# Streamed columns, additions per coefficient step and the order of dilated weight groups in a kernel of four layers

## What is computed

```python
fq, fk, fv, fg, dq, dk, dv = split(rms_norm(h) @ w_in)
fox_o = forgetting_attention(fq, fk, fv, fg + forget_bias)        # 16 heads of 64
dil_o = dilated_attention(rope(dq), rope(dk), dv)                 # 16 heads of 64
h = h + concat(rms_norm(fox_o), rms_norm(dil_o)) @ w_out
q = (hn @ w_query).reshape(T, 8, 2, 128)                          # hn = rms_norm(h)
scores = einsum('thpc,hpnc->thpn', q, sub_keys)                   # 128 keys for each half
...                                                               # best 16 pairs (i1, i2) of each of 8 heads
experts = i1 * 128 + i2                                           # 128 experts for each token
u = take(expert_down, experts); hdn = gelu(einsum('ted,td->te', u, hn))
y = einsum('te,ted->td', gates * hdn, take(expert_up, experts))
out = rms_norm(h + y)
```

## Time and profile before

| | us |
|---|---|
| median of three runs | 3365.07 |
| the three runs | 3365.07, 3355.38, 3365.72 |
| profiled execution | 3357.47 |
| its span | 3355.6 |
| TensorE busy in the span | 2604.7 (78%) |
| VectorE busy | 2260.8 (67%) |
| ScalarE busy | 1014.9 (30%) |
| GpSimd busy | 829.3 (25%) |
| HBM traffic | 255 GB/s mean |

### The profile page before, as it was taken

One profiled execution on the slowest core, in us unless ns is written; L12 is line 12 of the kernel. 1 busy time (PEld: TensorE's weight loads), 2 busy tenths in 40 slices (PEclk: granted clock), 3 DMA queues, 4 the chain that ended last, 5 costly groups with the idle time before them and its releaser, 6 DMA issues.

```text
span 3355.6 us, 34774 instructions
## 1 busy us (share of the span) xinstructions
PE 2604.7 (78%) x13316; PEld 2045.2 (61%) x13316; DVE 2260.8 (67%) x3034; ACT 1014.9 (30%) x1651; POOL 829.3 (25%) x581
## 2 busy tenths in 40 slices
PE   3789999998989999799999893000097029999998
PEld 3689999987879877798887793000064016544443
DVE  6777777776755455443544558999999984566666
ACT  2133434343444444443335540000086014200000
...
DMA  8767777776856534365342455999999993699998
GB/s 292 250 226 256 268 266 255 265 247 215 279 176 171 145 113 140 94 183 150 112 121 76 139 164 241 371 359 349 357 421 421 422 368 113 240 409 410 409 409 332
DMA packets 340693, 858.35 MB, mean 256 GB/s; under 512 B 38072, under 2 KB 97728, under 8 KB 306864
## 3 DMA queue, kind: packets, MB, share of 16 engines
...
HBM read 853.95 MB, written 2.10 MB: 255 GB/s over the span
## 4 chain that ended last, share of the span: by engine, by line
PE 38%; DVE 13%; DMA 12%; POOL 9%; issue 3%; ACT 1%; DVEq 0%; ACTq 0%; POOLq 0%
DMA s<-in_up_rows,s 11%; PE ps L1718 10%; PE ps L1719 10%; PE ps L1720 10%; POOL s L627 9%; DVE s L1663 7%; PE ps L2226 2%; DVE s L1676 1%; PE ps L2204 1%; PE ps L2202 1%; PE ps L2095 1%; DMA s<-in_peer_down,s 1%; PE ps L1979 1%; POOL s L639 1%; PE ps L2097 1%
## 5 line engine op out<-in xcount | busy, mean ns | idle before, releaser
L1718 PE MATMUL ps<-r,r 128*128 128x256 f32 (+2 forms) x3248 | 1064.7, 328 | 76.2 <-DVE r L1066 45.0
L1066 DVE TENSOR_TENSOR r<-s,r 128x1024 fp32r<-128x1024 f32 (+1 forms) x532 | 649.6, 1225 | 588.8 <-ACT r L654 588.5
L1719 PE MATMUL ps<-r,r 128*128 128x256 f32 (+2 forms) x3248 | 1045.5, 322 | 0.0
L1720 PE MATMUL ps<-r,r 128*128 128x256 f32 (+2 forms) x3248 | 1045.2, 322 | 0.0
L654 ACT CAST r<-s 128x1024 fp32r<-128x1024 f32 (+1 forms) x532 | 551.3, 1039 | 916.6 <-PE ps L1720 870.3
L1718 PEld LDWEIGHTS ps<-r,r 128*128 128x128 f32 x3248 | 640.4, 197 | 130.6 <-DVE r L1066 43.0
L1719 PEld LDWEIGHTS ps<-r,r 128*128 128x128 f32 x3248 | 640.4, 197 | 42.7 <-issue 4.5
L1720 PEld LDWEIGHTS ps<-r,r 128*128 128x128 f32 x3248 | 639.4, 197 | 40.8
L1663 DVE CUSTOM_DVE_ANT_0 s<-s,s 128x2048 f32<-128x2048 f32 x256 | 583.7, 2285 | 30.6 <-DMA s<-in_peer_down,s 30.3
L627 POOL DMA_INDIRECT s<-in_peer_down,s x256 | 472.8, 1847 | 398.5 <-DVE s L1621 187.9
L1676 DVE SCALAR_TENSOR_TENSOR s<-s,s,s 128x1024 f32<-128x1024 f32 x256 | 328.5, 1283 | 164.9 <-DMA s<-in_up_rows,s 163.2
...
...
## 6 DMA issues: line engine op xcount, KB each, us to landing
...
s<-in_ret_w_in SPq DMA_DIRECT2D x128, 512.0 KB, 5.2
s<-in_up_blocks SPq DMA_DIRECT2D x128, 512.0 KB, 6.8
...
s<-in_ret_w_in SPq DMA_DIRECT2D x128, 256.0 KB, 3.9
...
```

Of the source, the lines that this page charges most:

```text
L1066: v.tensor_tensor(lo_of(w), raw_of(w), hi_of(w).bitcast(F), ALU.subtract).then_inc(*lo_made.to(w))
L1718: pe.matmul(o, lh, rh, start=start, stop=False, skip_group_check=True)
L1719: pe.matmul(o, lh, rl, start=False, stop=False, skip_group_check=True)
L1720: return pe.matmul(o, ll, rh, start=False, stop=stop, skip_group_check=True)
```

## The change

**Experts.** DCOL goes from 1024 to 896: each up gather brings 1152 columns for 1024, each block 896, in matmuls of 448. There are five gather buffers for six; four block buffers stay, and both sets lie elsewhere: two block buffers lie where the indices were, so the first blocks wait for the indices' rounded and transposed copies, and the first two gather buffers lie in the selection's scratch. For t = 1 the comparison is made for the first index alone. The second index is transposed once for the tile and negated into SECOND, and ScalarE makes OH2 from it and a table of 0 to 127 with four small activations a step. Two additions go with a step.

**Dilated groups.** They are computed in the order 0, 2, 4, 1, 3, 5. X rounds call next once each, and L rounds 0 to 7 once each, two units a round. The four turns move to L rounds 8 and 9, two each, and the 16 O3 units to rounds 9 to 20, one or two each.

```diff
@@ constants and buffers @@
-DCOL = 1024
-NU = 6
+DCOL = 896
+HCOL = DCOL // 2
+NU = 5
...
-        EFR = [at(kept_end + 256 * t, 2, 128, of=arena_r) for t in range(2)]
+        EFR = [at(kept_end + 256 * t, 2 - t, 128, of=arena_r) for t in range(2)]
+        SECOND = at(kept_end + 384, 128)
...
-        ubuf = [at(144 * KB + 1024 * i, D - DCOL) for i in range(2)] + [at(YG + 1024 * i, D - DCOL) for i in range(4)]
-        sbuf = [at(W + 4096 + DCOL * i, DCOL) for i in range(NS)]
+        ubuf = [at(W + 4096 + (D - DCOL) * i, D - DCOL) for i in range(2)] + [at(YG + (D - DCOL) * i, D - DCOL) for i in range(3)]
+        sbuf = [at(144 * KB + DCOL * i, DCOL) for i in range(2)] + [at(W + 8192 - DCOL * i, DCOL) for i in (2, 1)]
...
+        DIL_ORDER = (0, 2, 4, 1, 3, 5)
...
-        for g in range(6):
+        for g in DIL_ORDER:
             cols512(w2, 3088 + g * 512)
...
+        def fox_units(i):
+
+            each = (0,) * 9 + (1, 2, 1, 2, 1, 2, 1, 2, 1, 1, 1, 1)
+            return range(sum(each[:i]), sum(each[:i + 1])) if 0 <= i < 21 else ()
@@ sync @@
             sp.wait_ge(*gate_made.at(1))
+            sp.wait_ge(*picks_rounded.at(1))
+            sp.wait_ge(*second_copied.at(0))
             for b in range(128):
@@ gpsimd @@
+            g.wait_ge(*gate_made.at(1))
             for n in range(256):
                 i, t, j = n % NU, n // 128, n % 128
-                if n == 0:
-                    g.wait_ge(*picks_rounded.at(1))
-                elif n == 2:
+                if n == 2:
                     g.wait_ge(*rows_used.at(255))
@@ scalar: dilated part @@
-            for i in range(21):
+            for i in range(22):
                 if i < 16:
                     exps("L", i)
                 if 0 <= i - 1 < 16:
                     flip_copy("L", i - 1)
+                if i < 8:
+                    next(work)
                 if i == 1:
                     mix_part(0)
-                if 2 <= i < 6:
-                    turn("O", i - 2, colA[:, 88:104], None, HT)
-                if i >= 6:
-                    cast(O3 + 4 + i - 6)
+                if i in (8, 9):
+                    for _ in work:
+                        pass
+                    turn("O", 2 * i - 16, colA[:, 88:104], None, HT)
+                    turn("O", 2 * i - 15, colA[:, 88:104], None, HT)
+                for u in fox_units(i - 1):
+                    cast(O3 + 4 + u)
@@ scalar: experts @@
             for t in range(2):
+                if t:
+                    s.wait_ge(*second_turned.at(0))
+                    s.mul(SECOND, bank[5][:, 0:128], -1.0).then_inc(*second_copied.to(0))
...
-                        s.wait_ge(*compared.at((t, q)))
-                        if 32 * t + q >= 2:
-                            s.wait_ge(*built.at(fours[32 * t + q - 2]))
-                        if t == 0:
+                        if t:
+                            s.wait_ge(*second_copied.at(0))
+                            s.wait_ge(*built.at(fours[30 + q]))
+                            for k in range(4):
+                                c = 4 * q + k
+                                r = s.activation(OH2[q % 2][:, k, :], STEP, ACT.Abs, bias=SECOND[:, c:c + 1])
+                            r.then_inc(*less_read.to((t, q)))
+                        else:
+                            s.wait_ge(*compared.at((t, q)))
+                            if q >= 2:
+                                s.wait_ge(*built.at((0, q - 2)))
                             s.activation(flat(o1), bank[q % 2], ACT.Abs)
-                        s.activation(o2, bank[2 + q % 2], ACT.Abs).then_inc(*less_read.to((t, q)))
+                            s.activation(o2, bank[2 + q % 2], ACT.Abs).then_inc(*less_read.to((t, q)))
@@ vector: experts @@
-                if 2 <= n < 34:
-                    q = n - 2
+                if n % 2 and n // 2 - 1 in range(32):
+                    q = n // 2 - 1
@@ tensor: dilated part @@
                     next(work, None)
                 if 0 <= i - 1 < 16:
                     flip("X", i - 1)
-                if i < 16 and i % 2:
-                    next(work, None)
                 if i >= 2:
                     attend("X", i - 2, FV)
-            for _ in work:
-                pass
-            pe.wait_ge(*rotated.at(("D", 7)))
-            pe.wait_ge(*dv_copied.at((1, 1)))
...
             for i in range(21):
+                if i in (0, 8):
+                    if i:
+                        for _ in work:
+                            pass
+                    pe.wait_ge(*rotated.at(("D", 7 if i else 3)))
+                    pe.wait_ge(*dv_copied.at((i // 8, 1)))
                 if i < 16:
                     scores_of("L", i, DQ, DK)
+                if i < 8:
+                    next(work)
...
-                if 2 <= i < 6:
-                    turn("O", i - 2, O, lambda t, k: mix_normed.at((t, 0)))
-                if i >= 5:
-                    out_unit(O3 + i - 5, (i - 5) // 4, (i - 5) % 4)
+                if i in (8, 9):
+                    turn("O", 2 * i - 16, O, lambda t, k: mix_normed.at((t, 0)))
+                    turn("O", 2 * i - 15, O, lambda t, k: mix_normed.at((t, 0)))
+                for u in fox_units(i):
+                    out_unit(O3 + u, u // 4, u % 4)
@@ tensor: experts @@
-                for p in range(2):
+                for p in range(2 - t):
                     b = 2 * p + q % 2
...
             for t in range(2):
+                if t:
+                    take(5)
+                    pe.transpose(bank[5][:, 0:128], EF[1][:, 1, :], IDN).then_inc(*second_turned.to(0))
+                    free[5] = second_copied.at(0)
                 compare(t, 0)
...
-                        r = pe.matmul(bank[2 * t + b], coef_of(t, i2), sbuf[i2 % NS][:, b * 512:(b + 1) * 512],
+                        r = pe.matmul(bank[2 * t + b][:, 0:HCOL], coef_of(t, i2), sbuf[i2 % NS][:, b * HCOL:(b + 1) * HCOL],
                                       start=i2 == 0, stop=i2 == 127)
```

75 lines of the change are left out of this document (37 added, 38 removed).

## The result

The changed kernel takes 3310.35 us (median of 4 runs, 3309.86 to 3310.61) against 3364.36 (median of 4 runs, 3355.38 to 3365.72): ratio 0.9845, interval 0.9828 to 0.9862. It is 54 us faster, and the time lies inside the forecast's range.

A forecast was written before the change was run, and what follows sets the result against it. Two chains were taken to end together: TensorE's blocks and gathers in the remaining DMA bandwidth. Parts one to three -57 us, part four -5: span 3293.6, plus 2 and 3.5, predicted 3299 us; range 3281 to 3334.

The forecast's parts named there:

- Part one: Coefficient steps: 4.60 us falls to 3.46, set by VectorE, TensorE next at 3.16; dense product starts 27 us earlier.
- GpSimd ... is done in 2.8: Coefficient step: GpSimd's two gather issues need 0.94 us each, and even at a 1.39 pace end in 2.8 us.
- the 2 us granted for refilling: Coefficient steps: 2 us added to 31 x 3.46 = 107 us for refilling five gather buffers.
- Part two: Dense product: TensorE's block shrinks from 3.43 to 3.00 us, 384.5 us for 128, ending at 3260.
- Part three: Up gathers: 2.30 us each beside blocks, 1.65 for the last 19; last addition about 3283 instead of 3339.6.
- rival 4: Up gathers: rows of 4608 bytes travel as two packets, 20 us added, 3319 us in all; chance 0.05.
- Part four: Dilated groups: spread units fill the sparse stretch at the first L heads; -5 us taken, bounds -12 and +12.
- Rival 5: Dilated groups: spread units cost instead of giving, by more frequent half clock in X; 3312 us, chance 0.07.
- The 3.5 us added: Whole kernel: 3.5 us added to 3295.5, since the profiled execution lay 8 us below the median of three runs.
- The sum: Whole kernel: 3355.6-57-5 = 3293.6 us span, 2 us around it, 3295.5 for an execution like the profiled one.
- rival 6: After the blocks, additions at 1.5 us, dilated groups give 12: 3290 us, or 3283 with more GB/s; chance 0.06.

The follow-up runs named there:

- e3: Changed kernel with one addition per coefficient step instead of two: 3346.05 us.
- e2: Kernel before with only the dilated groups' new order put in, experts untouched: 3354.85 us, ratio to before 0.9974.
- e10: Changed kernel with 928 streamed columns, first_hot cut in halves, and two of the first four blocks loaded ahead of the new waits: 3283.58 us, ratio to before 0.9766.
- e8: Changed kernel with 928 streamed columns instead of 896, nothing else: 3292.52 us, ratio to before 0.9789.
- e1: Changed kernel with the dilated groups in their old order, experts' change kept: 3321.15 us, ratio to before 0.9875.

## Why the prediction was right, and where it was off

**Part one.** TensorE's step without the second comparison: forecast 3.16, e3 shows 3.09. (The 4.60 us from which it was worked out was one step; the mean of the 31 before was 4.48. The working's 2752.1+30x4.6+1 meets the 2891 read in the trace although there are 31 steps.) VectorE's 3.46 is in the trace to the hundredth, but only in steps without a wait; the mean is 3.71. The step that failed is "GpSimd ... is done in 2.8": it took the pace of six additions in a row, 1.39 us, as GpSimd's pace, while in the changed kernel an issue takes 1.45 us and 0.30 follow, 3.5 in all, so that there is almost no reserve to make up for a late landing. Its row stood in the earlier trace rows: in 2455 to 2727 us GpSimd is busy 238.14 us for 110 issues, 2.17 us each and not 0.94, beside VectorE's products of the down rows. Price: 31 x 0.25 less the 2 us granted for refilling, 6 us on both chains.

**From the last step to the dense product** it took 10.9 us, not the 9.4 of before: the gain matmuls (2872.98, above) took 7.16 us. They took 7.16 or 7.17 in the other twelve kernels' traces too, also behind steps without a gap (e3) and with the experts of before (e2). The execution profiled of before is the exception:

```profile
2895.59 4.94 PE L2234 MATMUL ps<-s 16*128 16x128 f32 x32 [0.94 <-ACT s L1003]
```
```profile
2894.60:2898.00 3.40, 2.46 (x22) 2.44 (x22) 3.19 (x3) 0.65 (x2) 2.71 (x3) 1.00 0.58 164
```

The granted clock was 1.00 for these 3.4 us there, and 0.50 in every other trace. So the forecast took a lucky 9.4 for the rule; from the last first_hot to these matmuls the changed kernel takes 0.8 us less (3.77 instead of 4.54), so that 1.5 us are left of the 2.2.

**Part two.** Right: blocks of 3.007 us, 387.4 us for all where 386.5 were forecast, clock 1.00, TensorE 25 us ahead of the gathers (23 forecast).

**Part three.** Right in kind: 409 GB/s, landing 9.7, an end set by the gathers alone. From the last step to the last addition 423.7 us where 419 were forecast. The pace beside the blocks is right: 163 additions in 376.0 us, from the first block streamed again (2885.7) to the landing of the last (3261.7), are 2.31 each, 2.30 forecast. The two ends, where the gathers have the DMA engines alone, were mis-sized: 9 additions in the 16.5 us after the last step, 1.8 each instead of 1.6, and 18 in 31.2 us behind the last block's landing, 1.74 instead of 1.65, again with issues of 1.2 to 2.1 us (3276.09, above). And the last block landed 5.8 us before TensorE's end, not 9. Of these 18 additions, 14 come after TensorE's end, where some 20 were forecast. Rows of 4608 bytes were not cut: 20,912 packets of that queue in 2900 to 3235 us, for 146 gathers of 128 rows and their closing packets (a ninth), so rival 4 falls.

**Part four.** The trace gives 4.9 us for X and L together (298.3 us instead of 303.2 from X's first scores to L's last product), 5 were forecast. Of these 3.1 were lost again before the first addition. About half, 1.4 us, lies between L's last product and the first product of the down rows, which is 197.5 us or more in every trace with the new order and 195.9 and 196.3 in the two with the old one. The other 1.7 us lie in the stretch of the down rows, by the blocks now loaded at 2575 us in full DMA traffic. The forecast had put that load at nothing; e10, which loads two of the four at 2393 us, has that stretch 1.9 us shorter than e8. In the new order X and L took 298.3 or 298.4 us in each of the twelve traces; in the old one 303.2 in the execution of before and 310.8 in e1's, where 217 us of X ran at a clock of 0.92 and of 0.88:

```profile
1554.00:1771.00 217.00, 217.00 (x1291) 186.14 (x1291) 92.60 (x181) 75.56 (x137) 0.00 (x0) 0.92 0.39 114
```
```profile
1554.00:1771.00 217.00, 217.00 (x1253) 186.34 (x1252) 89.76 (x179) 73.08 (x133) 0.00 (x0) 0.88 0.36 107
```

That would explain why the groups are worth 8.7 to 10.8 us against the median, while only 1.6 us lie between the profiled executions of before and e2 (3357.5 and 3355.8): the profiled one of before lay 7 us under the median. It isn't shown, since no median execution of before was profiled. Nor does the new order make all executions alike: the changed kernel's four lie within 0.8 us, but e2's eleven spread over nearly 9 us and e3's four over 7.3, and 10 was the spread of before. Rival 5 did not come: the clock in X was 0.91 or 0.92 in the new order. The 3.5 us added to come from the profiled execution to the median were too much: the changed kernel's profiled execution is within 0.3 us of its median.

**The sum** in the profiled execution: forecast span 3293.6, measured 3308.8. Of the 15 us, 4 stem from the start of the steps (part four's gain lost on the way), 6 from the steps, 5 from the gathers before and behind the streamed blocks; the 1.5 of the gain matmuls is on TensorE's chain alone, which had room. The 3.5 us added for the median go the other way, which leaves the 11.

Three slips of the working changed nothing: 34 additions are done at the last step of before, not 35; rival 5 at the stated bound of +12 instead of -5 would be 3316, not 3312; and the range 3281 to 3334 does not leave out rival 6, whose 3290 and 3283 lie in it.
